# Four placements in a two-block fp32 kernel: dot pieces of the recurrent stage, one scatter, the router's logits, the last scatter

## What is computed

```python
# first block, layer 1: recurrent layer on h (256 x 1024), D_RNN = 1536
z = h @ w_in; xr, gate = split(z, 2)
xr = centred_depthwise_conv(xr, conv_w, conv_b)
y = rg_lru(xr, forward) + rg_lru(xr, backward)     # gates: 16 blocks of 96, then a scan over time
y = (y * gelu(gate)) @ w_out
# beside it, for later layers: mod = silu(c) @ ada_w + ada_b
# second block: mixture of experts, 16 experts in 4 groups, the best group and 2 experts in it per token
probs = softmax(h @ router_w); sel = probs + router_b
for e in range(16):
    he = (silu(h @ w_gate[e]) * (h @ w_up[e])) @ w_down[e]
    out = out + combine[:, e:e + 1] * he
x = x + mod[5] * out
return rmsnorm(x, final_norm_g)                    # x * rsqrt(mean(x*x) + eps) * g
```

## Time and profile before

| | before |
|---|---|
| median of 3 runs | 1385.08 us (1382.33 to 1387.37) |
| the profiled execution | 1385.05 us |
| its span in the profile | 1383.6 us |
| busy: PE, DVE, ACT | 1301.6, 1022.7, 706.2 us |
| HBM read | 305.82 MB |
| mean granted TensorE clock | 0.971 of full speed |

### The profile page before, as it was taken

The page is one execution under the profiler, slowest core; times in us unless marked ns, Lnnn a source line. Parts: engine busy times, 40 slices in busy tenths (PEclk is TensorE's granted clock), DMA queues, the critical chain, the costliest instruction groups (busy, mean ns, idle before and its releaser), DMA issues.

```text
span 1383.6 us, 20164 instructions
## 1 busy us (share of the span) xinstructions
PE 1301.6 (94%) x7922; PEld 1169.6 (85%) x7922; DVE 1022.7 (74%) x1462; ACT 706.2 (51%) x968; POOL 0.4 (0%) x5
## 2 busy tenths in 40 slices
PE   6988999999998899999999899998999999999996
PEld 6877899999887788999998688998888878878774
DVE  5667776877667897878877858775768679687685
ACT  3432445453367773554453643332557567576563
POOL 0000000000000000000000000000000000000000
PEclk9968999999999999999999999999899999999998
DMA  8718787777276666766762632220458879788772
GB/s 337 265 68 324 273 322 290 258 290 259 106 282 236 239 248 234 264 240 250 269 231 78 209 130 92 92 63 11 162 181 310 304 234 346 251 295 292 231 260 84
DMA packets 82686, 308.19 MB, mean 223 GB/s; under 512 B 9312, under 2 KB 9568, under 8 KB 81824
## 3 DMA queue, kind: packets, MB, share of 16 engines
q1 hardware_dynamic: 80352, 292.59, 59.1%
q10 hardware_dynamic: 2240, 14.31, 2.6%
HBM read 305.82 MB, written 1.05 MB: 222 GB/s over the span
## 4 chain that ended last, share of the span: by engine, by line
PE 77%; DVE 14%; DMA 4%; ACT 4%; issue 2%; ACTq 0%; DVEq 0%; SPq 0%
PE ps L465 76%; DMA ring<-stream 4%; DVE junk L424 2%; DVE w_low L424 2%; ACT w_high L424 1%; DVE ti L424 1%; DVE rs L424 1%; PE ps L1131 1%; DVE hsc L424 1%; DVE t_two L424 1%; ACT ta L424 1%; DVE y_experts L424 1%; DVE x_low L424 0%; DVE sc L424 0%; DVE t_one L424 0%
## 5 line engine op out<-in xcount | busy, mean ns | idle before, releaser
L424 DVE TENSOR_TENSOR w_low<-ring,w_high 128x1024 fp32r<-128x1024 f32 x368 | 442.5, 1223 | 139.6 <-ACT w_high L424 136.8
L424 ACT ACTIVATE w_high<-ring 128x1024 fp32r<-128x1024 f32 x368 | 387.0, 1060 | 294.8 <-PE ps L465 170.5
L465 PE MATMUL ps<-x_high,w_high 128*128 128x256 f32 (+1 forms) x816 | 239.6, 294 | 18.1 <-DVE x_low L424 11.7
L465 PE MATMUL ps<-x_high,w_low 128*128 128x256 f32 (+1 forms) x816 | 236.1, 289 | 0.0
L465 PE MATMUL ps<-x_low,w_high 128*128 128x256 f32 (+1 forms) x816 | 235.9, 289 | 0.0
L424 DVE CUSTOM_DVE_ANT_0 junk<-ring,cond 128x1024 f32<-128x1024 f32 x137 | 166.9, 1223 | 33.3 <-DMA ring<-stream 24.5
L465 PEld LDWEIGHTS ps<-x_high,w_high 128*128 128x128 f32 x816 | 156.3, 192 | 25.5 <-DVE w_low L424 11.5
L465 PEld LDWEIGHTS ps<-x_low,w_high 128*128 128x128 f32 x816 | 155.9, 191 | 1.6
L465 PEld LDWEIGHTS ps<-x_high,w_low 128*128 128x128 f32 x816 | 155.3, 190 | 1.8
L465 PE MATMUL ps<-h_high,w_high 128*128 128x256 f32 x512 | 145.3, 284 | 6.8 <-DVE h_low L424 4.8
L465 PE MATMUL ps<-h_high,w_low 128*128 128x256 f32 x512 | 145.4, 284 | 0.0
(11 more groups left out here) (320 smaller groups left out, 1965.0 us busy)
## 6 DMA issues: line engine op xcount, KB each, us to landing
ring<-stream SPq DMA_DIRECT2D x364, 512.0 KB, 5.2
ring<-moe SPq DMA_DIRECT2D x192, 512.0 KB, 4.9
gw<-gw ACTq DMA_DIRECT2D x1, 3840.0 KB, 15.7
tab_two<-tab ACTq DMA_DIRECT2D x1, 2824.0 KB, 15.5
cond<-cvec ACTq DMA_DIRECT2D x2, 512.0 KB, 5.6
x<-xT ACTq DMA_DIRECT2D x1, 1024.0 KB, 12.0
ctx_first<-ctxT ACTq DMA_DIRECT2D x1, 1024.0 KB, 4.6
ctx<-ctxT ACTq DMA_DIRECT2D x1, 1024.0 KB, 4.8
```

The lines of the kernel that those rows point to most:

```text
L424: return op(*a, **k).then_inc(self.sem, by)
L465: return pe.matmul(out, stationary, moving, start=start, stop=stop, skip_group_check=True)
```

## The change

It has four parts.

1. `RNN_CHUNKS`: the tiles with two chunks are 2, 3, 4, 5 and no longer 3, 5, 8, 10. The number of dot pieces stays.
2. `SCATTERS`: the rounds of place 0 stand at the gate of expert 15 and no longer at that of 14.
3. The router's logits are made as 16 x 256 (router columns stationary, 256 tokens moving, 8 matmuls), copied by ACT, and turned to two tiles of 128 x 16 by two PE transposes after the fourth of the 16 turns of x.
4. The last scatter uses banks 6, 7, 0, 1, so no round waits for DVE; six `keep_on` matmuls stand before and six after it; ACT multiplies x with the final gain (8 instructions of 128x256, between and behind its squares), and DVE's last step is two products of 128x1024 in place of eight of 128x256.

```diff
-RNN_CHUNKS = {("z", t): 2 if t in (3, 5, 8, 10) else 1 for t in range(2, NT)} | {("o", t): 1 for t in range(5)}
+RNN_CHUNKS = {("z", t): 2 if t in (2, 3, 4, 5) else 1 for t in range(2, NT)} | {("o", t): 1 for t in range(5)}
...
-SCATTERS = {7: 1, 12: 2, 14: 0}
+SCATTERS = {7: 1, 12: 2, 15: 0}
+LAST_BANKS = (6, 7, 0, 1)
...
     for k in range(KT):
         pe.wait_ge(s.x_high, x_splits(MOD_MOE) + k + 1)
-        for b in range(2):
-            ins = mm(PS[:, 4 + b, 0:NE], m.T2[:, k, b * P:(b + 1) * P], m.par("rw", k * NE, NE), k == 0, k == KT - 1)
-    ins.then_inc(s.rlogit, 1)
+        ins = mm(PS[0:NE, 7, 0:256], m.par("rw", k * NE, NE), m.T2[:, k, :], k == 0, k == KT - 1)
+    ins.then_inc(s.rrow_mm, 1)
     for b in range(2):
         for k in range(KT):
+            if (b, k) == (0, 4):
+                pe.wait_ge(s.rrow, 1)
+                for h in range(2):
+                    ins = pe.transpose(PS[:, 4 + h, 0:NE], m.ROUT[0:NE, 760 + h * P:760 + (h + 1) * P], m.ident[0:NE, 0:NE])
+                ins.then_inc(s.rlogit, 1)
             ins = mm(PS[:, 2 * b + k // 4, (k % 4) * P:(k % 4 + 1) * P], m.T2[:, k, b * P:(b + 1) * P], m.ident, k % 4 == 0, False)
...
-        if r >= 2 or at > 0:
+        bank = LAST_BANKS[r] if i == 3 else 6 + r % 2
+        if bank >= 6 and (r >= 2 or at > 0):
             pe.wait_ge(s.x_add, X_MOE + 8 * at + 2 * (r - 2) + 2)
...
+    keep_on(6)
     for r in range(4):
         scatter(3, r)
+    keep_on(6)
     square_sums(SQ_END, m.SUM_END, m.T2, KT)
...
+    act.wait_ge(s.rrow_mm, 1)
+    A(m.ROUT[0:NE, 760:1016], PS[0:NE, 7, 0:256], ACT.Copy, s.rrow, apart=True)
...
-    rms_rows(m.X, KT, m.T2, D, 10, (s.x_add, X_MOE + 26, 2), m.SUM_END)
+    def with_gain(blocks):
+        for k in blocks:
+            A(m.XFIN[:, k, :], m.X[:, k, :], ACT.Copy, s.x_gain, scale=m.par("fing", k), apart=True)
+
+    for r in range(4):
+        act.wait_ge(s.x_add, X_MOE + 26 + 2 * r)
+        A(m.T2[:, 2 * r:2 * r + 2, :], m.X[:, 2 * r:2 * r + 2, :], ACT.Square, s.sq, apart=True)
+        if r in (1, 2):
+            with_gain((2 * r - 2, 2 * r - 1))
+    with_gain((4, 5, 6, 7))
+    root(10, m.RSTD, m.SUM_END, 1.0 / D, "eps6")
...
-    for k in range(KT):
-        op(vv.scalar_tensor_tensor, m.X[:, k, :], m.X[:, k, :], m.par("fing", k), m.RSTD, ALU.mult, ALU.mult, inc=s.final, apart=k > 0)
+    for half in range(2):
+        vv.wait_ge(s.x_gain, 4 * half + 4)
+        blocks = slice(4 * half, 4 * half + 4)
+        op(vv.tensor_tensor, m.X[:, blocks, :], m.XFIN[:, blocks, :], m.RSTD.unsqueeze(1).broadcast_to([P, 4, S]), ALU.mult, inc=s.final, apart=half > 0)
```

More of the change, by code:

```diff
@@ L197 @@
     hy_tr vt2 dft_mm dft inv_mm yv mixed fa_mm fa fl_mm fy fn_mm
-    rlogit rmax rexp go cnt order onehot diag comb_w cw_mm cw db_mm scat xt_mm xt xg_mm xg_high xg_low
-    silu h ht_mm e_high e_low y_out y_add sc_mm final
+    rrow_mm rrow rlogit rmax rexp go cnt order onehot diag comb_w cw_mm cw db_mm scat xt_mm xt xg_mm xg_high xg_low
+    silu h ht_mm e_high e_low y_out y_add sc_mm x_gain final
 """)
@@ L242, in __init__ @@
         self.XF = kt(view("x_whole", aX, 2048))
-        self.MEAN, self.VAR, self.SUM_END, self.RSTD = PS[:, 4, 0:256], PS[:, 5, 0:256], PS[:, 0, 0:256], self.RS[:, 0:256]
+        self.MEAN, self.VAR, self.SUM_END, self.RSTD = PS[:, 4, 0:256], PS[:, 5, 0:256], PS[:, 2, 0:256], self.RS[:, 0:256]
         self.combo, self.gate1 = self.MISC[:, 16:80], self.MISC[:, 96:104]
@@ L349, in __init__ @@
         self.YES = tuple(rounded("y_experts_" + n, a, 2048).rearrange("p (a d) -> p a d", a=2) for n, a in (("high", aT2), ("low", aB + 5120)))
+        self.XFIN = kt(view("x_final", aB + 5120, 2048))
         self.YS = tuple(rounded("y_single_" + n, a, 1024) for n, a in (("high", aT1 + 1024), ("low", aT1)))
@@ L454, in load_program @@
     for half in range(2):
-        sp.wait_ge(s.final, 4 * half + 4)
+        sp.wait_ge(s.final, half + 1)
         sp.dma_start(outT[:, 4 * half:4 * half + 4, :], m.X[:, 4 * half:4 * half + 4, :]).then_inc(s.out, 16)
@@ L1155, in scatter @@
         pe.wait_ge(s.y_add, Y_LOW[i] - (i > 0 and r < 2))
-        if r >= 2 or at > 0:
+        bank = LAST_BANKS[r] if i == 3 else 6 + r % 2
+        if bank >= 6 and (r >= 2 or at > 0):
             pe.wait_ge(s.x_add, X_MOE + 8 * at + 2 * (r - 2) + 2)
         for d in (2 * r, 2 * r + 1):
-            out, blk = PS[:, 6 + r % 2, (d % 2) * 256:(d % 2 + 1) * 256], slice(d * P, (d + 1) * P)
+            out, blk = PS[:, bank, (d % 2) * 256:(d % 2 + 1) * 256], slice(d * P, (d + 1) * P)
             if i == 0:
@@ L2405, in results @@
         for d in (2 * r, 2 * r + 1):
-            add_branch(d, PS[:, 6 + r % 2, (d % 2) * 256:(d % 2 + 1) * 256], m.MOD[:, 136 + d:137 + d])
+            add_branch(d, PS[:, LAST_BANKS[r] if i == 3 else 6 + r % 2, (d % 2) * 256:(d % 2 + 1) * 256], m.MOD[:, 136 + d:137 + d])
     low_upto(W_MOE + 12)
```

## The result

The changed kernel took 1371.31 us (median of 4 runs, 1369.43 to 1371.86) against 1385.36 for the kernel before (4 runs); the ratio is 0.991, 95% interval 0.9892 to 0.9928. The forecast was 1372.5, 1.2 us above it. The profiled executions have spans of 1383.6 and 1370.4 us, 13.2 apart.

A forecast was written before the change was run, and what follows sets the result against it. PE, busy 1301.6 of 1383.6 us, bounds the kernel, so only its waits, half clock or removable work pay. -9.4 - 2.4 - 0.9 + 0.1 = -12.6 on 1385.05 gives 1372.5 us; the forecast's own range is 1367 to 1377.

The forecast's parts named there:

- z(9,0) and o(0): Recurrent stage: waits of 3.91 and 4.40 us before these pieces go, with the half clocks behind them (1.76 and 1.79).
- New waits: Recurrent stage, at z(3,0), z(4,0) and z(6,0): added waits of 1.7 us together, from 0.3 to 3.5.
- DVE next: Recurrent stage: DVE is late next, gaining 10.3 us by itself; middle of 10.3 and 11.86 taken, 11.1.
- 11.86: Recurrent stage: cost in us of both waits and half clocks at z(9,0) and o(0), 3.91 + 1.76 + 4.40 + 1.79.
- Part 2: Scatter of place 0, expert 14's gate: 7.5 gained, 3.8 given back, half clock loss taken; -2.4 us, between -5 and -1.
- I take this loss: Expert 14's gate: half clock behind the 2.4 us wait before the third piece, pieces and turn of 1.4 to 1.7 paid twice.
- Part 3: Router logits: gain of 0.9 us; nothing if a new PE gap brings half clock, +3 if ACT's copy holds turns up.
- Part 4: Last scatter and norm: root 1.0 us later, last products 0.9 shorter; +0.1 in sum, between -1 and +1.4.
- The drain: Before the root at the end: skill's 1.38 us per table switch would make the sum -11.2; left out, following the trace.
- part 1: Dots at tiles 2 to 5, recurrent stage: -11.1 + 1.7 = -9.4 us, between -11.0 and about -6.
- The rivals: Ring waits return with half clock, 1378.3 us, 0.19; late dots hold DVE, 1381, 0.08; slower landings, 1394.8, 0.05.
- the first: Recurrent stage, tiles 3 to 6: ring waits come back with the half clock, 1378.3 us; chance 0.19.

## Why the prediction was right, step by step

- **z(9,0) and o(0): right.** Both waits went, both rows run at full clock. z(9,0) was issued at the end of tile 7's first dot and landed 0.3 us ahead of use; the text had 0.5. The run with four dots at tile 10 brought the second wait back alone, so that one is its own tile's doing. For z(9,0) the issue rows say the same; no run put four dots back at tile 8 alone.
- **New waits: right in place, 2.3 instead of 1.7 in sum.** z(3,0) 0.25, z(4,0) 0.27 and z(6,0) 1.56, the last by the train of five pieces that the text named (the last of them landed 8.8 us after the train began, the text had 8.4); 0.21 at an output piece wasn't foreseen. The run with the chunk at tile 6 took the 1.56 away and gave it to the stage.
- **DVE next: right.** 11.86 less 2.3 would be 9.6; the stage gave 8.69. The missing 0.9 (0.76 foreseen) lies in the output pieces; the largest piece is the 0.52 at 494.95, a wait for a landing that the kernel before doesn't have there. That wait doesn't set the end of the stage: PE still stands for the y behind it, 0.53 against 0.51 before, so without the late landing it would have stood longer there. VectorE is next in line as forecast.
- **What the 11.86 rest on.** They count the half clock behind both waits. In the five traces with the old table it came at o(0) five times and at z(9,0) four times. Against the second trace of the kernel before, where it was missing at z(9,0) and both waits were shorter, the stage of the changed kernel is 5.8 shorter and not 8.7. The removal of the waits is the change's; part of the size is that of the trace it was read from.
- **Part 2: size right, condition wrong.** The terms held to 0.1: 7.5 less 3.8, with a wait of 2.42 where 2.4 stood. That is partly luck, as the kernel before was itself 0.44 shorter here in its second trace. The step "I take this loss", the half clock behind the new wait, was the one that failed: in this trace the clock stayed at 1.00. Its reason was wrong too: 2.4 doesn't lie nearer to 3.91 than to one microsecond, and the loss put in the sum, 1.3, is below the 1.4 to 1.7 of the text. Of the six traces that have this wait, two (those of the runs that filled the router's idle time) show the half clock behind it, and there the stretch was 1.1 longer. The loss exists, but not each time.
- **Part 3: wrong by 1.8.** "I take 0.9 of gain": it was a loss of 0.9 in this trace. The count did start 0.63 earlier. The exponential no longer waits for VectorE, but starts 0.2 later than before against the rows ahead, where the text had it level. What failed is the clock: the text named a new gap on PE, ahead of the turns and at the price of the gain, and didn't take it. The gap came behind the turns, ahead of the count, and the half clock that had lain over the turns lay over the count and the gathering, where it cost the gain and 0.9 more. The five traces that have the new router without filling show 0.05 to 0.93 of loss; none shows a gain. With both gaps filled and the clock at 1.00 the router is 1.35 shorter in one run; in the other a half clock right behind it left nothing.
- **Part 4: right.** +0.1 was forecast, 0.0 measured. The root is 0.8 later (forecast 1.0), the products 0.9 shorter.
- **The drain:** the root's activation starts at 1362.85, 0.02 behind the end of the load, with ScalarE busy right up to the load. The drain that the Trainium skill ("ScalarE: Activation LUTs", section "What ACT_TABLE_LOAD costs") adds to a switch is not seen here, and the trace was the better guide.
- **Not in the sum at all:** two half clocks at places whose instructions no part touches, -1.52 and -1.34, against +0.64 and +0.52 of small waits elsewhere, together -1.7. With the misses of part 1 (+0.7), part 2 (-1.3), part 3 (+1.8) and part 4 (-0.1) that is -0.6: -12.6 forecast, -13.2 in the trace. That the total was nearer than its terms is luck.
- **The rivals.** None of the three took over. The waits of the first were there, but as short as the forecast had them and without the half clock. What speaks most against it is that in no run was a wait of 0.2 to 1.8 us in this stage followed by the half clock. That isn't a rule for other places. The prediction took no loss for waits of about a microsecond because it had looked at this stage and at one long window; in the same trace of the kernel before, waits of 1.52 at 785.61 and of 1.50 at 1358.67 were followed by the half clock.

What stays open is what decides whether a wait of 1.5 to 3.7 us is followed by the half clock. The traces show that it is neither its length alone nor the instructions ahead of it (768); nothing here varied its place in time on purpose.

## What to carry to other kernels

Where pieces come through a ring in fixed order, read the issue times against the releases: a burst of pieces for another engine delays whichever critical piece stands behind it, and moving the burst to a place where the critical pieces go out well before it gives the whole wait back. When work is moved away from a wait, ask what still stands ahead in the other engine's queue: the split of place 0 went on costing 2.4 us though nobody near needed it. And treat the half clock behind waits as a chance with a price, worked out apart from the sum, look for it over the whole trace and not only at the longest waits, and fill the idle time with matmuls of a measured length where the wait can't be removed.

## What the runs showed of the hardware

- An idle TensorE of 3.63 us was followed by full clock and one of 2.05 by the half clock, in two traces of the same kernel. Behind one and the same wait of 2.62 us near 768, with the same instructions up to it, it came in three of five traces. Behind a wait of 1.5 us near 785 it came in 13 of 14.
- A stretch of matmuls of ones kept the granted clock at 1.00 through both of the router's waits in each of the two runs that had it.
- Two samples of one kernel (8 and 11 runs) had a ratio of 1.003 with an interval of 1.0009 to 1.005, and single times of the kernel before spread from 1377 to 1389 us. With such events of 1.3 to 1.6 us each, a change of 2 us is better read from the two traces, stretch by stretch, than from the total.
